# Pool layer of an mLSTM/pooling trunk: group mix multiplied into the input weights, input projection by Strassen with 7 products, output projection accumulated over all of K in PSUM

## The chip, the core and the metric

The kernel runs on one core of one Trainium2 chip. The metric is device time in microseconds (us). Of the kernel before there are three timed executions: 1609.27, 1611.42 and 1612.48 us, median 1611.42. One further execution was profiled. It took 1616.39 us, and its span from the first to the last instruction is 1614.3 us. All rows below are from that one.

## What is computed

```python
def _pool_branch(x, w_in, w_group, scale, w_out):      # layer 1; S = D = 1024, E_B = 2048
    proj = x @ w_in                                    # (1024, 1024) @ (1024, 4096)
    u, z = proj[..., :E_B], proj[..., E_B:]
    csum = jnp.cumsum(u, axis=1)
    for gi, win in enumerate((2, 4, 8, 16)):           # 4 groups of 512 channels
        cg = csum[..., gi * CG_B:(gi + 1) * CG_B]
        means.append((cg - prev) / cnt)                # trailing mean over win tokens
    pooled = concatenate(means) - u
    mixed = einsum("bsgc,gcd->bsgd", pooled, w_group) * scale    # 512 x 512 for each group
    return (mixed * silu(z)) @ w_out                   # (1024, 2048) @ (2048, 1024)

# x <- LayerNorm(alpha * x + branch(x)), layer 0 (mLSTM, 8 heads) first, then this one
```

The window mean acts along tokens and the group mix along channels, so the two can change places.

## The kernel before, in words

TensorE works on float32 data in three passes: each operand is split into a rounded part (`_hi`, type fp32r, made by ScalarE) and a remainder (`_lo`, made by GpSimd or VectorE), and `split` (L1388 to L1392) issues hi times hi, lo times hi and hi times lo. So a product of 128 x 128 weights with 512 columns is three matmuls.

Layer 0 (mLSTM) runs head by head. Its last output projection, the LayerNorm between the layers and the first products of the pool layer are interleaved in TensorE's queue by the table `BRIDGE` (L74): T are transposes of the last head's output, O the 16 last output products of layer 0, X the 16 groups of four transposes that bring the normed input back to channels on partitions, U the first two input products.

The pool layer then goes through its four groups (`group`, in the blocks of TensorE, VectorE and ScalarE). For each group TensorE makes 4 + 4 blocks of the input projection (u and z, each 128 channels by 2 x 512 tokens by 8 K tiles), the group mix (`G_MIX`), and the output projection of the group's 512 channels (`project`, L1429), whose partial sums VectorE adds to `acc` in SBUF (L962). Weights arrive in slots of 128 x 1024 floats in a ring of two: DMA to `w_raw`, ScalarE to `w_hi` (L646), GpSimd to `w_lo` (L541). Four PSUM banks (`wide`) rotate. VectorE makes the window sums (L1303: four levels for every group, those not wanted multiplied by a flag of zero), the pooled value (L1310), its remainder (L1315), the gate (L1324) and the gated product (L1337).

The last group's projection goes token tile by token tile. As each tile is done, its LayerNorm passes through VectorE (L1210, L1364), ScalarE (sum of squares L822, scaling L938), GpSimd (L570, L572, L636) and out. The two last tiles are finished by VectorE (L1369).

Each engine's order is the order in which its block of code issues; there is no planner. Waits are semaphores. On VectorE every instruction that feeds the next waits on a semaphore of its own (`step`, `link`).

Of the kernel before, what the change touches and what calls it, by code (L numbers as in the profile page):

```python
# [84 lines left out]
SLOTS_PER_HEAD = 8
SLOT_LAST_OUT = SLOTS_PER_HEAD * HEADS - 2
SLOT_POOL = SLOTS_PER_HEAD * HEADS
SLOTS_PER_GROUP = 14
# [6 lines left out]
G_U, G_Z, G_MIX, G_OUT = 0, (8, 16), (12, 36), (20, 40)  # L95
GS_U, GS_Z, GS_MIX, GS_OUT = 0, (4, 7), (6, 11), (9, 12)
# [12 lines left out]
VEC_BETWEEN, VEC_GROUP = 2, 20  # L109


SET_IDENT, SET_PAR, CONST_SETS = 2, 4, 14
POOL_SETS = 4 + 3 * GROUPS + sum(win - 1 for win in WINDOWS)
LATE = NC - 2
# [32 lines left out]
def group_uses(g):  # L147
    return Uses(g * USES_PER_GROUP + USE_POOL, g * (USES_PER_GROUP // 4) + USE_POOL // 4)


def build(nc, x, w_in, conv_w, conv_b, w_q, w_k, w_v, b_i, b_f, norm_g, skip, w_out,
          p_in, p_group, p_scale, p_out, ln_g, ln_b, out):
    m_rows = nc.dram_tensor("m_rows", (HEADS, S), F32, kind="Internal").ap()
    wc_rows = nc.dram_tensor("wc_rows", (HEADS, NC), F32, kind="Internal").ap()
    with ExitStack() as ctx:
# [17 lines left out]
        sb("line_0", [P, (BASE - CONSTS - SMALLS) // 4])  # L173
        with ExitStack() as behind:
            normed_out = sb("normed_out", [P, NC, D], where=behind)
        x_hi = sb("x_hi", [P, KT, S], F32R)
        x_lo = sb("x_lo", [P, KT, S], F32R)
        acc = sb("acc", [P, NC, D])
        w_raw = sb("w_raw", [P, 2, SLOT])
        w_hi = sb("w_hi", [P, 2, SLOT], F32R)  # L180
        w_lo = sb("w_lo", [P, 2, SLOT], F32R)
        gate_t = sb("gate_t", [P, 2, HALF])


        with ExitStack() as gates:
            e_buf = sb("e_buf", [P, 2, S], where=gates)
            f_buf = sb("f_buf", [P, 2, S], where=gates)
        y_hi = sb("y_hi", [P, 2, S], F32R)
        y_lo = sb("y_lo", [P, 2, S], F32R)


        with ExitStack() as own:
            def sa(name, shape, dt=F32):
                return sb(name, shape, dt, own)
            xm = sa("xm", [P, 2, HALO + S])
            sa("line_1", [P, (LINE - 32) // 4])

            with ExitStack() as whole:
                xc = sb("xc", [P, 2, S], where=whole)
            xc_lo = sa("xc_lo", [P, 2, S], F32R)  # L200
# [178 lines left out]
        def by_feature_tile(k):  # L379
            return bank(k).rearrange("p (f t) -> p f t", f=4)  # L380
# [1280 lines left out]
```

## Time and profile before

| | |
|---|---|
| median of 3 timed executions | 1611.42 us |
| profiled execution, its time | 1616.39 us |
| its span | 1614.3 us |
| PE busy | 1558.9 us (97%) |
| DVE, ACT, POOL busy | 1044.3, 491.4, 429.6 us |
| mean granted TensorE clock | 0.986 |

PE is TensorE, DVE VectorE, ACT ScalarE, POOL GpSimd, SP the engine that issues the transfers. A matmul's record is longer than its share of the engine, because matmuls overlap: how fast TensorE goes is read from the distance between starts. Records carry start, duration, engine, line, output, inputs; brackets give the idle time before and what ended it. A granted clock of 1 is 2.4 GHz, and half of it 1.2 GHz.

### The profile page before, as it was taken

The page shows a single profiled execution, that of the slowest core. Times are in us where ns is not written, and L with a number is a line of the kernel's source. Part 1 is how long each engine was busy: PE and PEld are TensorE (multiplying, and loading weights), DVE is VectorE, ACT ScalarE, POOL GpSimd, SP SyncE. Part 2 cuts the span into 40 slices and gives each one's busy share as a digit, 9 for nine tenths or more (in the row PEclk, how much of TensorE's full clock was granted, in tenths as well). Part 3 has the DMA queues.
Part 4 walks back from the last instruction along what each step waited for, and adds up shares of the span by engine and source line. Part 5 has one row for each costly group of instructions (what it writes and reads, how often), then busy time and mean ns, then how long its engine had stood idle before and what let it go on. Part 6 is the DMA issues. An engine that isn't in the chain of part 4 may idle for free.

```text
span 1614.3 us, 20693 instructions
## 1 busy us (share of the span) xinstructions
PE 1558.9 (97%) x7186; PEld 1295.1 (80%) x7186; DVE 1044.3 (65%) x1507; ACT 491.4 (30%) x711; POOL 429.6 (27%) x260
## 2 busy tenths in 40 slices
PE   7999999999999999999999879899999999999995
PEld 6888888888888888888888758678888888888884
DVE  4868757567577477576675787855563565348348
ACT  4632332422422332323224243221221123112214
POOL 2203202213122123132032153452122222212226
PEclk8999999999999999999999999999999999999998
DMA  5112111201112112021111021111111111111113
GB/s 173 47 34 64 42 40 52 60 31 52 52 30 61 39 39 65 26 65 50 28 52 52 0 66 40 39 53 40 53 53 49 43 52 52 39 52 52 41 50 119
DMA packets 108509, 82.59 MB, mean 51 GB/s; under 512 B 4120, under 2 KB 96424, under 8 KB 108464
## 3 DMA queue, kind: packets, MB, share of 16 engines
q1 hardware_dynamic: 107392, 81.94, 17.1%
q8 instruction: 26, 0.43, 0.1%
q10 hardware_dynamic: 1072, 0.07, 0.0%
q14 instruction: 19, 0.16, 0.0%
HBM read 77.77 MB, written 4.23 MB: 51 GB/s over the span
## 4 chain that ended last, share of the span: by engine, by line
PE 85%; DVE 11%; ACT 1%; issue 1%; DMA 1%; POOL 1%; DVEq 0%; SPq 0%; ACTq 0%; POOLq 0%
PE wide L1390 26%; PE wide L1391 26%; PE wide L1392 26%; PE ps_intra L1540 2%; PE ps_state L1545 1%; PE ps_inter L1543 1%; DVE win_b L1303 1%; DVE normed_out L1364 1%; PE wide L1447 1%; PE ps_s L1533 1%; DVE acc L1291 1%; DVE win_a L1303 1%; DVE tmp_a L1048 1%; DVE acc L1210 1%; DVE x_lo L969 0%
## 5 line engine op out<-in xcount | busy, mean ns | idle before, releaser
L541 POOL TENSOR_TENSOR w_lo<-w_raw,w_hi 128x1024 fp32r<-128x1024 f32 x120 | 311.7, 2597 | 854.0 <-ACT w_hi L646 852.6
L1390 PE MATMUL wide<-x_hi,w_hi 128*128 128x512 f32 x1280 | 507.5, 396 | 10.1 <-POOL w_lo L541 10.1
L1392 PE MATMUL wide<-x_hi,w_lo 128*128 128x512 f32 x1280 | 500.6, 391 | 0.0
L1391 PE MATMUL wide<-x_lo,w_hi 128*128 128x512 f32 x1280 | 500.0, 391 | 0.0
L1390 PEld LDWEIGHTS wide<-x_hi,w_hi 128*128 128x128 f32 x1280 | 241.3, 189 | 59.0 <-POOL w_lo L541 11.2
L1392 PEld LDWEIGHTS wide<-x_hi,w_lo 128*128 128x128 f32 x1280 | 241.0, 188 | 50.8
L1391 PEld LDWEIGHTS wide<-x_lo,w_hi 128*128 128x128 f32 x1280 | 241.2, 188 | 47.9
L962 DVE TENSOR_TENSOR acc<-wide,acc 128x512 f32<-128x512 f32 x224 | 154.8, 691 | 98.7 <-PE wide L1392 86.0
L1390 PE MATMUL wide<-w_hi,y_hi 128*128 128x512 f32 x512 | 202.2, 395 | 10.7 <-DVE y_lo L1032 4.8
L1391 PE MATMUL wide<-w_lo,y_hi 128*128 128x512 f32 x512 | 200.8, 392 | 0.0
L1392 PE MATMUL wide<-w_hi,y_lo 128*128 128x512 f32 x512 | 200.7, 392 | 0.0
L646 ACT ACTIVATE w_hi<-w_raw 128x1024 fp32r<-128x1024 f32 x120 | 127.4, 1062 | 186.8 <-PE wide L1392 179.2
L1390 PEld LDWEIGHTS wide<-w_hi,y_hi 128*128 128x128 f32 x512 | 97.0, 189 | 34.4 <-DVE acc L1210 6.5
L1392 PEld LDWEIGHTS wide<-w_hi,y_lo 128*128 128x128 f32 x512 | 97.0, 189 | 20.6
L1391 PEld LDWEIGHTS wide<-w_lo,y_hi 128*128 128x128 f32 x512 | 96.9, 189 | 19.7
L547 POOL TENSOR_TENSOR rstd<-small,nhalf 128x4 f32<-128x4 f32 x16 | 16.1, 1009 | 281.5 <-DVE small L1137 281.5
L1048 DVE SCALAR_TENSOR_TENSOR tmp_a<-xm,cols,tmp_a 128x1024 f32<-128x1024 f32 x48 | 72.0, 1500 | 5.6 <-DVE acc L962 0.3
L1324 DVE SCALAR_TENSOR_TENSOR zz<-gate_t,wide 128x512 f32<-128x512 f32 x32 | 22.0, 687 | 82.0 <-ACT gate_t L882 81.2
L1303 DVE SCALAR_TENSOR_TENSOR win_b<-win_a,flag 128x1024 f32<-128x1024 f32 x32 | 73.1, 2284 | 1.6 <-DVE win_a L1303 0.2
L802 ACT ACTIVATE num<-ps_intra 128x257 f32<-128x257 f32 x64 | 24.8, 387 | 107.1 <-PE ps_state L1545 78.7
L1390 PE MATMUL wide<-p_hi,w_hi 128*128 128x512 f32 x128 | 50.4, 394 | 2.2 <-DVE zz L1324 2.2
L724 ACT ACTIVATE tmp_c<-tmp_a 128x1024 f32<-128x1024 f32 x16 | 17.0, 1062 | 116.8 <-DVE tmp_a L1048 116.8
(182 smaller groups left out, 1967.6 us busy)
## 6 DMA issues: line engine op xcount, KB each, us to landing
w_raw<-in_mlstm_w_in SPq DMA_DIRECT2D x48, 512.0 KB, 3.8
w_raw<-in_pool_w_in SPq DMA_DIRECT2D x32, 512.0 KB, 3.8
w_raw<-in_mlstm_w_out SPq DMA_DIRECT2D x16, 512.0 KB, 3.8
w_raw<-in_pool_w_out SPq DMA_DIRECT2D x16, 512.0 KB, 3.8
acc<-in_x SPq DMA_DIRECT2D x8, 512.0 KB, 6.0
m_bc<-m_rows SPq DMA_DIRECT2D x8, 512.0 KB, 4.7
w_raw<-in_pool_w_group SPq DMA_DIRECT2D x8, 512.0 KB, 3.4
out<-normed_out SPq DMA_DIRECT2D x6, 512.0 KB, 2.6
```

The costliest lines, as they stand in the source:

```text
L541: link(pool, pool.tensor_tensor(w_lo[:, k % 2, :], w_raw[:, k % 2, :], w_hi[:, k % 2, :].bitcast(F32), ALU.subtract), lo_ready, s + 1)
L646: link(act, act.activation(w_hi[:, k % 2, :], w_raw[:, k % 2, :], ACT.Copy), hi_ready, s + 1)
L724: link(act, act.activation(tmp_c[:, :], tmp_a[:, :], ACT.Tanh), conv_tanh, h * 2 + (j + 1))
L802: link(act, act.activation(num[:, c, :], ps_intra[:, 0:DV + 1], ACT.Copy), intra_taken, h * NC + (c + 1))
L962: link_taken(dve, dve.tensor_tensor(acc[:, t, half(n)], bank(k), acc[:, t, half(n)], ALU.add), uses, k)
L1048: ins = dve.scalar_tensor_tensor(out=tmp_a[:, :], in0=xm[:, j, w:w + S], scalar=col(h * 2 + (COL_W + w * ET + j)), in1=tmp_a[:, :], op0=AL ...
L1303: step(dve.scalar_tensor_tensor(out=dst[:, PAD:PAD + S], in0=src[:, back:back + S], scalar=flag[:, bass.ds(g * GROUPS + level, 1)], in1=sr ...
L1324: link_taken(dve, dve.scalar_tensor_tensor(out=zz[:, m // 2, half(m % 2)], in0=gate_t[:, m % 2, :], scalar=1.0, in1=bank(k), op0=ALU.add, ...
L1390: pe.matmul(dst, a[0], b[0], start=first, stop=False)
L1391: pe.matmul(dst, a[0], b[1], start=False, stop=False)
L1392: return pe.matmul(dst, a[1], b[0], start=False, stop=last)
L1540: mm = pe.matmul(ps_intra[:, 0:DV + 1], sT[:, :], v_sb[:, c, :], start=True, stop=True)
```

## The change

1. The group mix is not applied to the pooled data any more. Between the layers TensorE multiplies each group's u part of `pool_w_in` by `w_group` (32 steps "F" of 12 matmuls). The result is evicted by ScalarE to `stage` and written to a DRAM tensor `folded`. The F steps stand in a new `BRIDGE` table between T, O and X.
2. The input projection, u with folded weights and z as before, is 16 pairs of 256 channels by 1024 tokens by K = 1024, each a 2 x 2 block product by Strassen's scheme: 7 products of 12 matmuls in place of 8. Odd pairs are u, even ones z. The sums of weight blocks are made by GpSimd (4 additions of 128 x 512 for each pair), those of x blocks by VectorE, once. M1 (q = 1) is accumulated on in its bank, with copies (snapshots) taken by ScalarE; VectorE joins a second bank to a copy three times for each pair.
3. The window sums take as many levels as the window needs (1 to 4), without a flag. The gated y goes to DRAM (`y_rows`) and comes back by token halves.
4. The output projection runs after all pairs, with all 16 K tiles accumulated in PSUM: 4 token tiles, then 3, then the last one alone with both operands resident. The LayerNorm after it is on VectorE, with only the square root on GpSimd.

The core of the diff:

```diff
+BRIDGE = [("T", 0), ("T", 1), ("F", 0), ("F", 1), ("F", 2), ("T", 2), ("T", 3), *(("O", i) for i in range(8)), ("F", 3),
+          *(("O", i) for i in range(8, 12)), ("X", 0), ("X", 1), ("O", 12), ("X", 2), ...
+PRODUCTS = [(0, 1), (0, 2), (0, 6), (0, 7), (0, 5),
+            *((p - back, q) for p in range(1, PAIRS)
+              for back, q in ((0, 1), (1, 3), (0, 2), (1, 4), (0, 6), (0, 7), (0, 5))),
+            (PAIRS - 1, 3), (PAIRS - 1, 4)]
...
 @block.gpsimd
+            fold_low(3)
+            for t in range(2):
+                deviation(t, 0)
+            fold_low(4)
+            for t in range(2, 4):
+                deviation(t, 0)
...
+            def add(dst, a, b, n):
+                link(pool, pool.tensor_tensor(dst, a, b, ALU.add), added, n)
+            for p in range(PAIRS):
...
+                add(blk_sum_at(AT[p, 7]), a_part(p, 0), a_part(p, 2), 4 * p + 1)
+                add(blk_sum_at(AT[p, 6]), blk_sum_at(AT[p, 7]), a_part(p, 3), 4 * p + 2)
+                pool.wait_ge(blk_lo, AT[p, 2] + 1)
+                add(a_part(p, 1), blk_sum_at(AT[p, 6]), a_part(p, 1), 4 * p + 3)
...
+                add(blk_sum_at(AT[p, 5]), a_part(p, 2), a_part(p, 3), 4 * p + 4)
 @block.scalar
+            for t in range(3):
                 sum_squares(t, 0, squares_a)
...
+            for c in range(4):
+                fold_take(0, c)
+            sum_squares(3, 0, squares_a)
+            for s in (4, 5):
+                fold_high(s)
 @block.vector
+            def join(p, q):
...
+                dve.tensor_tensor(dst, wide[:, at, :], dst, op).then_inc(done, 1)
...
+            def windows_at(t):
+                for p in range(1, PAIRS, 2):
+                    start = AT[p, 3] - 1
+                    ops = p // 4 + 4
+                    for j in range(2):
+                        for n in range(ops):
+                            if start + 2 + 4 * j + n * 5 // ops == t:
+                                window(p, j, n)
...
+            for t in range(TICKS):
+                tick(t)
+            for t in range(TICKS, TICKS + RING + 2):
+                windows_at(t)
...
+            for k in range(ET):
+                wo_low(k)
+                y_low(k)
 @block.tensor
+            def fold_free(b, c):
+                if b == 0:
...
+                elif b in (1, 3):
+                    by, count = formed(4 * b + c)
+                    pe.wait_ge(x1_taken[by], count)
+            def bank_ready(p, q):
+                if q == 1 and p >= 2:
...
+                elif q in (6, 5, 3):
+                    pe.wait_ge(snap, 3 * p + {6: 1, 5: 2, 3: 3}[q])
+                elif q == 2 and p:
+                    pe.wait_ge(c11, p)
+                elif q == 7 and p:
+                    pe.wait_ge(c21, p)
+                elif q == 4:
+                    pe.wait_ge(c22, p + 1)
+            for i, (p, q) in enumerate(PRODUCTS):
+                pe.wait_ge(blk_lo, i + 1)
...
+            for v in range(2 * ET):
+                k, ts = v % ET, range(4, LATE) if v >= ET else range(4)
+                if v < ET:
+                    pe.wait_ge(wo_lo, k + 1)
+                pe.wait_ge(y_half_lo, v + 1)
```

Three places in the queues, first GpSimd between the layers. L570 and L572 (before) and L782 and L784 (now) are the two steps of one token tile's LayerNorm deviation. Before, small memsets stand between them:

```order
L570 TENSOR_SCALAR small<-small 128x1 [waits ln_squares,pool_set]
L572 TENSOR_TENSOR rstd<-small,nhalf 128x1 [waits ln_var]
L589 MEMSET head_fix 128x1 [waits ln_rstd]
L589 MEMSET head_fix 128x1 [waits pool_set] x8
L570 TENSOR_SCALAR small<-small 128x1 [waits ln_squares,pool_set]
```

Now, for tiles 0 to 3:

```order
L782 TENSOR_SCALAR small<-small 128x1 [waits ln_squares,fold_lo0]
L784 TENSOR_TENSOR rstd<-small,nhalf 128x1 [waits ln_var]
L782 TENSOR_SCALAR small<-small 128x1 [waits ln_squares,ln_rstd]
L784 TENSOR_TENSOR rstd<-small,nhalf 128x1 [waits ln_var]
L754 TENSOR_TENSOR fold_w<-fold_raw,fold_w 128x1024 [waits fold_hi,ln_rstd]
L782 TENSOR_SCALAR small<-small 128x1 [waits ln_squares,fold_lo0]
```

A remainder of fold weights (fold 4), which waits for ScalarE, now stands ahead of the deviations of tiles 2 and 3.

Next ScalarE at the same time. Before, with L822 the sum of squares of a token tile, L711 the rounding of the last head's y, L831 the eviction of an X step, L843 its rounding, L646 the rounding of a weight slot:

```order
L822 ACTIVATE tmp_a,small<-acc,small 128x1024 x2
L711 ACTIVATE y_hi<-tmp_c 128x512 x2
L822 ACTIVATE tmp_a,small<-acc,small 128x1024 x4
L831 ACTIVATE x_new<-ps_s,cols 128x512
L843 ACTIVATE x_hi<-x_new 128x512 x4
L646 ACTIVATE w_hi<-w_raw 128x1024
```

Now. L1041 is the sum of squares of a token tile (three, then one), L1072 the eviction of the first four fold tiles, L932 the rounding of fold weights (folds 4 and 5):

```order
L1041 ACTIVATE tmp_a,small<-acc,small 128x1024 x3
L1072 ACTIVATE stage<-ps_s 128x512
L1072 ACTIVATE stage<-ps_intra 128x512
L1072 ACTIVATE stage<-ps_inter 128x512
L1072 ACTIVATE stage<-ps_state 128x512
L1041 ACTIVATE tmp_a,small<-acc,small 128x1024
L932 ACTIVATE fold_w<-fold_raw 128x1024 x2
```

The rounding for fold 4 has come to stand behind the fold evictions and behind the sum of squares of tile 3.

Last VectorE where a group's data becomes ready for the output projection. Before (the last group, second half): the gated products and their remainders, and straight behind them the gate of the next z blocks and the additions of TensorE's projection:

```order
L1032 TENSOR_TENSOR y_lo<-y_t,y_hi 128x512 [waits y_rounded,wide_taken2]
L1337 SCALAR_TENSOR_TENSOR y_t<-wide,cols,zz 128x512 [waits wide_full,y_ready]
L1032 TENSOR_TENSOR y_lo<-y_t,y_hi 128x512 [waits y_rounded,wide_taken3]
L1032 TENSOR_TENSOR y_lo<-y_t,y_hi 128x512 [waits y_rounded,y_ready]
L1324 SCALAR_TENSOR_TENSOR zz<-gate_t,wide 128x512 [waits z_tanh,y_ready]
```

Now, behind the last product and its `join`, the second half of the windows of pair 15 (L1620 sums, L1624 first tokens, L1626 pooled, L1633 gated; the first half, the same seven, stands ahead of it), and then the first remainders of the output projection's weights (L1671) and of y (L1677):

```order
L1620 TENSOR_TENSOR win_a<-u_buf 128x1024 [waits c22,c21,y_made]
L1620 TENSOR_TENSOR win_b<-win_a 128x1024 [waits vec_step]
L1620 TENSOR_TENSOR win_a<-win_b 128x1024 [waits vec_step]
L1620 TENSOR_TENSOR win_b<-win_a 128x1024 [waits vec_step]
L1624 TENSOR_TENSOR win_b<-win_b,head_fix 128x16 [waits vec_step]
L1626 SCALAR_TENSOR_TENSOR win_a<-win_b,u_buf 128x1024 [waits vec_step]
L1633 SCALAR_TENSOR_TENSOR zz<-win_a,cols,zz 128x1024 [waits gate_used,pooled]
L1671 TENSOR_TENSOR wo<-wo_raw,wo 128x1024 [waits wo_hi,y_made]
L1677 TENSOR_TENSOR blk<-blk_raw,blk 128x512 [waits y_half_hi]
```

The operands of the first output product have come to stand behind the last pair's 14 window instructions.

## Rows read from the trace of the kernel before

**Rows 1.** The page: busy time, share of the span, instructions.
```profile
PE 1558.9 (97%) x7186; PEld 1295.1 (80%) x7186; DVE 1044.3 (65%) x1507; ACT 491.4 (30%) x711; POOL 429.6 (27%) x260
```

**Rows 2.** Windows from head 7's end: PE, PEld, DVE, ACT, POOL busy, clock, DMA, GB/s.
```profile
917.25:1057.00 139.75, 114.94 (x501) 92.40 (x502) 116.52 (x140) 47.35 (x67) 64.24 (x81) 0.93 0.15 45
1057.00:1574.00 517.00, 517.00 (x2281) 427.48 (x2279) 274.63 (x289) 115.14 (x144) 129.50 (x52) 1.00 0.16 48
1574.00:1614.30 40.30, 21.84 (x85) 16.52 (x84) 35.71 (x53) 16.84 (x22) 27.08 (x23) 0.82 0.30 119
```

**Rows 3.** PE timeline, start and duration in us, around the layers' border.
```profile
917.25 1.09 PE L1447 MATMUL wide<-ident,num 128*128 128x128 f32 x8 [0.38 <-DVE num L1144]
923.11 0.77 PE L1390 MATMUL wide<-w_hi,y_hi 128*128 128x512 f32 x1 [4.77 <-DVE y_lo L1032]
923.67 0.63 PE L1391 MATMUL wide<-w_lo,y_hi 128*128 128x512 f32 x1
...
927.09 0.44 PE L1390 MATMUL wide<-w_hi,y_hi 128*128 128x512 f32 x1
...
1017.41 0.50 PE L1390 MATMUL wide<-x_hi,w_hi 128*128 128x512 f32 x1 [3.11 <-POOL w_lo L541]
```

**Rows 4.** PE timeline: two X steps (four transposes each), and the last matmul.
```profile
954.70 0.60 PE L1576 MATMUL ps_intra<-ident,acc 128*128 128x128 f32 x4
955.13 0.60 PE L1576 MATMUL ps_inter<-ident,acc 128*128 128x128 f32 x4
...
1599.54 0.39 PE L1392 MATMUL wide<-w_hi,y_lo 128*128 128x512 f32 x1
```

**Rows 5.** Groups by line: count, busy us, mean ns, idle before. DVE.
```profile
L962 DVE TENSOR_TENSOR acc<-wide,acc 128x512 f32<-128x512 f32 x224 | 154.8, 691 | 98.7 <-PE wide L1392 86.0
L1303 DVE SCALAR_TENSOR_TENSOR win_b<-win_a,flag 128x1024 f32<-128x1024 f32 x32 | 73.1, 2284 | 1.6 <-DVE win_a L1303 0.2
L1094 DVE TENSOR_TENSOR xc_lo<-xc,xc_hi 128x1024 fp32r<-128x1024 f32 x16 | 19.6, 1225 | 0.5
```

**Rows 6.** Groups by line, POOL and ACT.
```profile
L541 POOL TENSOR_TENSOR w_lo<-w_raw,w_hi 128x1024 fp32r<-128x1024 f32 x120 | 311.7, 2597 | 854.0 <-ACT w_hi L646 852.6
L596 POOL TENSOR_TENSOR x_lo<-x_new,x_hi 128x512 fp32r<-128x512 f32 x8 | 10.8, 1349 | 8.9 <-ACT x_hi L843 8.7
L646 ACT ACTIVATE w_hi<-w_raw 128x1024 fp32r<-128x1024 f32 x120 | 127.4, 1062 | 186.8 <-PE wide L1392 179.2
L822 ACT ACTIVATE tmp_a<-acc,small 128x1024 f32<-128x1024 f32 x8 | 9.2, 1153 | 15.7 <-DVE small L1216 15.6
```

**Rows 7.** VectorE's timeline in group 0.
```profile
989.29 3.30 DVE L1303 SCALAR_TENSOR_TENSOR win_b<-win_a,flag 128x1024 f32<-128x1024 f32 x1
992.62 1.29 DVE L1303 SCALAR_TENSOR_TENSOR win_a<-win_b,flag 128x1024 f32<-128x1024 f32 x1
```

**Rows 8.** GpSimd's timeline: one deviation between the layers, and the same stretch.
```profile
932.73 0.19 POOL L570 TENSOR_SCALAR small<-small 128x1 f32<-128x1 f32 x1 [5.20 <-ACT tmp_a L822]
933.00 0.56 POOL L572 TENSOR_TENSOR rstd<-small,nhalf 128x1 f32<-128x1 f32 x1
...
989.06 2.44 POOL L541 TENSOR_TENSOR w_lo<-w_raw,w_hi 128x1024 fp32r<-128x1024 f32 x1 [6.17 <-ACT w_hi L646]
```

**Rows 9.** VectorE's timeline between the layers, and its last record.
```profile
927.83 1.76 DVE L1144 TENSOR_SCALAR num<-num,mv,small 128x256 f32<-128x256 f32 x4
...
1608.77 3.12 DVE L1369 SCALAR_TENSOR_TENSOR normed_out<-normed_out,rstd,b_bc 128x512 f32<-128x512 f32 x4
```

**Rows 10.** DMA issues: size, median us from issue to landing.
```profile
w_raw<-in_mlstm_w_in SPq DMA_DIRECT2D x48, 512.0 KB, 3.8
acc<-in_x SPq DMA_DIRECT2D x8, 512.0 KB, 6.0
out<-normed_out SPq DMA_DIRECT2D x4, 256.0 KB, 2.0
```

More of the change, by code:

```diff
@@ L108, with by_vector, fold_count @@
 VEC_START, VEC_FIRST, VEC_LATER = 4, 68, 58
[L109 to L114, printed above, removed]
+SET_IDENT, SET_PAR = 2, 4
+CONST_SETS = 14
+FIX_SETS = GROUPS + sum(win - 1 for win in WINDOWS)
+LATE = NC - 1
+def by_vector(s):
+    return s > 12 and s % 2 == 1
+def fold_count(s):
+    return sum(by_vector(i) == by_vector(s) for i in range(s + 1))
 def formed(n):
@@ L172, in build, with at_kb @@
         small = sb("small", [P, 4, NC])
[L173 to L189, printed above, removed]
+        head_fix = sb("head_fix", [P, GROUPS, PAD])
+        sb("line", [P, (BASE - CONSTS - SMALLS) // 4])
+        def at_kb(where, name, taken, kb):
+            assert taken <= kb * KB
+            sb(name, [P, int(kb * KB - taken) // 4], where=where)
         with ExitStack() as own:
@@ L564, in head @@
                     make_lo(s0 + (at["slots"] + f), f)
+                if last:
+                    for s in range(3):
+                        fold_low(s)
                 powers(1)
@@ new lines, in _ @@
+            dve.wait_ge(gb_last_in, 32)
+            for v in range(ET + AHEAD, 2 * ET):
+                y_low(v)
+                t = v - ET - AHEAD - 1
+                if 0 <= t < 4:
+                    norm_out(t)
+            for t in range(4, LATE):
+                for n in range(2):
+                    residual_in(2 * t + n, t, n)
+                mean(t, NC)
+            for t in range(4, LATE):
+                norm_out(t)
+            for n in range(2):
+                residual_in(2 * LATE + n, LATE, n)
+                step(dve.bn_stats(stats[:, n, :], acc[:, LATE, half(n)]))
@@ new lines, in _ @@
+            for i, (p, q) in enumerate(PRODUCTS):
+                pe.wait_ge(blk_lo, i + 1)
+                if i < 2:
+                    pe.wait_ge(x0_lo, 4 * i + 4)
+                elif p == 0:
+                    pe.wait_ge(x_lo_done, X_WAIT[q])
+                bank_ready(p, q)
+                dst = wide[:, {2: 2, 7: 3, 4: 3}.get(q, p % 2), :]
+                for t in range(4):
+                    mm = split(dst, [v[:, tile(t)] for v in (blk_hi_at(i), blk_lo_at(i))],
+                               [v[:, t, :] for v in operands[q]], t == 0 and q in (1, 2, 7), t == 3, q not in (1, 2, 7))
+                mm.then_inc(prod, 1)
```

1158 lines of the change are left out of this document (725 added, 433 removed).

## The prediction

> **What bounds the kernel now.** I read the page first: PE is busy 97% of the span, no other engine above 65% [rows 1]. So time is saved by fewer matmuls or by filling the places where PE waits. The windows by stage say where those are. I cut at 917.25, where the last head's products of layer 0 end; what lies before it the change leaves as it is, apart from some small GpSimd memsets and three early fold roundings that have cover. The middle stretch, 517 us, is full: 2281 matmuls, all but a few of 512 columns, or 0.2267 us each. The border between the layers (139.75 us) and the end (40.3 us) are not [rows 2]. From 917.25 to the end of the span are 697.05 us. TensorE's work in them: 2688 matmuls of the pool layer (1536 input, 384 mix, 768 output) at 0.2267 = 609.4; 96 of the last output products of layer 0 = 21.8; 16 X steps at 0.43 = 6.9 and 2.2 for the T transposes [rows 3, 4]; together 640.3. The last matmul ends near 1599.7, so 14.6 us are the tail behind it [rows 4]. The rest, 697.05 - 640.3 - 14.6 = 42.2, is waiting and half clock. The timeline shows both: 4.77 us of waiting at 923.11, and behind it nine matmuls 0.43 us apart (923.67 to 927.09, granted clock at its lower level, 1.2 GHz), which costs 9 x 0.2 = 1.8 us more. The wait of 3.11 us before 1017.41 was not followed by that [rows 3]. I price a wait of over 2 us with 1.3 us of clock on top, between the two.
>
> **The matmuls removed.** The group mix costs the same in both places: 32 F steps of 12 = 384 matmuls, because tokens and model width are both 1024. Output 768, as before. Input 112 products of 12 = 1344 in place of 1536. So 192 matmuls go: 192 x 0.2267 = **-43.5 us**.
> The Trainium skill, page "TensorE: Matmul & The Clock Gate", section "Wait — 56ns, not 53.3ns?", has 215.7 ns for a warm matmul of 512 columns; by it the saving would be 41.4 us. The trace does not agree for these operands, and its 0.2267 is used.
>
> **The border, new waits.** T0, T1 and F0 to F2 now cover the wait at 923.11 and end at 917.25 + 1.1 + 8.2 = 926.6; but T2 needs the second half of the normed output, ready at 927.83 + 1.76 = 929.6 [rows 9]: wait 3.0. Then T2, T3, eight O (10.9), F3 (2.7), four O (5.4): 949.9, where X0 stands. It needs token tiles 0 to 3 normed. GpSimd's queue has the remainder of fold 4 ahead of the deviations of tiles 2 and 3, and this waits for ScalarE, which first evicts F3 (to 945.2), then makes the sum of squares of tile 3 (1.15) and the rounding (1.06) [rows 6]: 947.5. GpSimd 2.6 more, two deviations of 0.19 + 0.56 [rows 8], and on VectorE a norm, two additions and a norm behind them (some 2.6): X0 at 954.4, wait 4.5. Queued behind that GpSimd instruction are both deviations, and all of TensorE waits for them. Around X8 to X15 ScalarE must evict block 2, round folds 14 and 15 and form X8 before X12 can overwrite its bank; fold 15 is fetched only when two evictions are done, lands 3.8 later [rows 10], is rounded in 1.06, and form X8 and X12 follow: some 7 us from the end of F11 to F12, with 3.4 of work in them: wait 4. The remaining F steps have four slots: landing 3.8 + rounding 1.06 + remainder 2.6 + use 2.72 + 0.6 of semaphores = 10.8 for the 10.9 us that four F steps take. That just holds; I give 0.6 us for each of seven blocks, 4.5. Sum 16.0, with clock for three of them 3.9: **19.9 us**.
>
> **The products.** PE needs 2.72 us for each of 112. VectorE's load for two pairs (38.1 us of PE): 14 remainders, 6 joins, 4 gates at 0.73 (0.69 and a gap) = 17.5, and the windows of the u pair: for each half g+1 sums at 1.27, 0.2 for the first tokens, two instructions at 1.32 [rows 5]. That is 25.7, 28.2, 30.8 and 33.3 us for groups 0 to 3: below 38.1, so on average it has room. But PE waits at one tight place: product (p+1, M7) overwrites the bank that `join` of (p, M4) reads, and only one product stands between. For z pairs this join is behind the windows. Counting VectorE's queue from the end of (p, M5) to that join, group 2: 4.6 + 2.7 + 3.1 + 2.8 + 0.7 = 14.0 us against 5 products = 13.6. One sum less for group 1, two for group 0; group 3 has 15.2. And in this stretch GpSimd makes its four additions of 1.3 us [rows 6].
> What does an addition cost VectorE? The window sum at 989.29 took 3.30 us where the next took 1.29; GpSimd was at a remainder from 989.06 to 991.50, and VectorE ended 1.09 behind that [rows 7, 8]. Over 32 such instructions the mean is 2284 ns [rows 5]. The additions that read PSUM keep 691 in the mean of 224 [rows 5]: these are not held. So bounds: none held, waits in all seven z pairs 0, 0, 0, 0, 0.4, 0.4, 1.6 = 2.4; all four held (5.2 us), 3.0, 3.0, 4.3, 4.3, 5.6, 5.6, 6.8 = 32.6. I take three of four held (3.9 us), since rows 7 show a full hold where VectorE is busy without a gap and one addition meets a join: 1.7 + 1.7 + 3.0 + 3.0 + 4.3 + 4.3 + 5.5 = 23.5. Clock for five of them 6.5; start of the stage (last fold stored, then blocks 4 and 5) 1.5: **31.5 us**.
> The Trainium skill, page "SBUF — State Buffer", section "Terms", says that VectorE and GpSimd share a port pair, that it is locked for the whole instruction and that the loser fully blocks. The trace agrees at 989.29. Taken for every addition it gives the upper end, which is a rival below.
>
> **Between products and output projection.** VectorE's queue holds, from the last product on: a join 0.73, 14 window instructions of pair 15 (8 x 1.27 + 2 x 0.2 + 4 x 1.32 = 15.9), then the first remainder of the output weights 1.27 and of y 0.73. TensorE waits for both, and nothing else is left for it: 18.6 + 0.3 + clock 1.3 = **20.2 us**. Bounds: GpSimd is silent here, so these are the unheld times; 17 to 22.
>
> **Output projection.** For each K tile TensorE takes 5.4 us; VectorE 1.27 + 0.73 + 2.6 (residual gain) = 4.6, ScalarE 1.06 + 0.63. PE stays full. The y tiles 14 and 15 are needed 76 us later. Nothing is late in the second half either. The 256 additions to `acc` that go (L962) were off the path.
>
> **The tail.** Before, it is bound by VectorE: each token tile there takes two additions and an L1364 of some 2.4 us, and VectorE is still at 1608.77 + 3.12 [rows 9]. Now only tile 7 is left: addition, statistics, variance, four normings of 128 x 512 at 0.69 to 0.78, some 5 us, and a transfer of 2.0 [rows 10] with 0.6 around: 7.6. **-7.0 us**.
>
> **Sum.** New waits 19.9 + 31.5 + 20.2 = 71.6 in place of 42.2: +29.4. -43.5 + 29.4 - 7.0 = -21.1. The profiled execution took 1616.39 (span 1614.3 and 2.1 around it), so 1595.3 on its scale. It stood 5.0 above the median of the runs, 1611.42; on their scale the forecast is **1590 us**.
>
> **Rivals.**
> A, the holds are hidden: GpSimd's additions fall where VectorE idles or reads PSUM. For it: VectorE has 5 to 12 us of room in two pairs. Against: the additions are released right at the window burst. Products wait 2.4, no clock there: 23.5 - 2.4 + 6.5 = 27.6 less, 1562.
> B, every addition holds VectorE in full: 32.6 and clock 9: 11.6 more, 1602.
> C, slower than before: the F steps are paced by their transfers. For it: loads of x with four in flight land in 6.0 us [rows 10], F steps need 512 KB every 2.72 us, and each block's stores go through the same queue, whose load of every fourth fold waits for two evictions. Chain 6.0 + 7.0 = 13.0 for four steps of 10.9: 2.1 x 7 = 15, and the queue's late fourth load 1.3 x 7 = 9 more: +24 and clock 2, 1616. It decides from a landing of about 4.0 us on. Against: before, 512 KB loads in the steady state land in 3.8.
> D, the change does not do what it says: PE does not keep 0.2267 in the products, since 12 matmuls alternate among four banks with seven waits for each pair, and 0.02 more on each of the 1344 eats 27 us: 1617. Rows 2 speak against it; before too a bank changed every 6 to 24 matmuls.
>
> **Chances.** Forecast 0.48, A 0.18, B 0.20, C 0.09, D 0.05. A difference below 0.2% (3.2 us) can't be told from none. Forecast and A are faster; of B and of the forecast's upper side a little reaches 1608; C and D split between no change and slower. Faster 0.84, same 0.06, slower 0.10. The range reaches from A's time to the upper side of B and the near side of C: 1562 to 1612.
>
> **What would show it.** In the profile of the changed kernel: one PE wait of 18 to 20 us ended by VectorE just ahead of the output projection; waits of 2 to 6 us ended by a VectorE join, once in every two pairs, growing with the group; GpSimd additions of 1.3 us beside window sums of over 2 us; X0 held some 4 us by a norm of VectorE; PE starts 0.2267 apart elsewhere; 8 us from the last matmul to the end. I am wrong if the products go without waits (A), if F steps wait for roundings one after the other (C), or if a wait that I have not priced stands before a stage, such as the first products waiting for x combinations.

## The result and the profile after

The changed kernel takes **1625.11 us** (median of 8 runs, 1616.91 to 1628.08), the kernel before 1610.66 beside it (8 runs, 1609.27 to 1614.52). The ratio is 1.0078, 95% interval 1.0058 to 1.0098: slower by 0.8%, where 1590 and faster had been forecast, and outside the range of 1562 to 1612. The profiled execution took 1626.17 us with a span of 1624.4; the forecast span was 1614.3 - 21.1 = 1593.2. So 31.2 us have to be explained.

First the page of the changed kernel, its busy lines (compare [rows 1]), and then windows of the same trace, cut at the first T step, the first product, the last product's end and the first output matmul. Their columns are those of [rows 2].

```profile
PE 1527.4 (94%) x6994; PEld 1265.0 (78%) x6994; DVE 1057.3 (65%) x1559; ACT 568.5 (35%) x850; POOL 385.9 (24%) x259
```
```profile
914.18:1090.95 176.77, 135.68 (x560) 108.43 (x561) 106.47 (x130) 84.61 (x109) 70.64 (x43) 0.86 0.45 137
1090.95:1422.63 331.68, 313.84 (x1345) 255.59 (x1343) 223.00 (x261) 124.39 (x201) 94.78 (x65) 0.98 0.25 83
1422.63:1441.06 18.43, 0.16 (x2) 0.03 (x1) 17.75 (x18) 9.41 (x11) 0.00 (x0) 0.62 0.98 398
1441.06:1624.40 183.34, 175.89 (x768) 144.93 (x768) 92.18 (x124) 34.91 (x50) 8.29 (x15) 0.98 0.20 69
```

The 192 matmuls are gone, 7186 - 6994, and yet the span grew. The third window is the bubble ahead of the output projection, with no work for TensorE. The first is the one that surprised: TensorE's work in it is 117.9 us by the durations of before, so 58.9 are lost, where 19.9 were forecast. Stage by stage against the prediction:

| | forecast | measured |
|---|---|---|
| layer 0 up to the first T step | 917.25 | 914.18 (-3.1) |
| lost at the border | 19.9 | 176.8 - 117.9 = 58.9 (+39.0) |
| lost in the products | 31.5 | 331.7 - 304.6 = 27.0 (-4.5) |
| bubble, with its clock | 20.2 | 18.4, and 1.6 of clock in the output stage (-0.2) |
| tail behind the last matmul | 7.6 | 7.6 |

-3.1 + 39.0 - 4.5 - 0.2 = +31.2. The miss lies wholly at the border. This is what TensorE waited for from the first T step on (line and operand waited for, total us, times, longest):

```profile
PE ps_s L1755 <- DVE blk L1677: 18.3, 1, 18.3
PE wide L1755 <- DVE zz L1594: 15.7, 7, 4.2
PE ps_s L1755 <- DVE fold_w L1511: 13.8, 2, 7.9
PE ps_s L1755 <- POOL fold_w L754: 10.7, 5, 6.2
PE ps_s L1936 <- DVE acc L1492: 5.4, 1, 5.4
PE ps_s L1936 <- ACT xa_raw L1048: 3.9, 1, 3.9
PE ps_s L1936 <- ACT stage L1072: 3.3, 1, 3.3
PE wide L1804 <- DVE num L1408: 3.2, 2, 2.8
...
```

The first two lines are the bubble and the seven joins, in the places that were forecast; the bubble has its size too (18.9 forecast), the joins are a third smaller (23.5). X0 (5.4 for 4.5) and T2 (2.8 for 3.0) are there too. Two lines hold what I had not priced: 13.8 us in two F steps that wait for VectorE, and 6.2 us of the fourth line at F0. What is left of that line, 4.5 us in four F steps, is as much as was forecast for the F steps.

**The two F steps.** The two are F27, which starts at 1064.25, and F29 at 1080.00. The chain that ended last runs to both by the same kinds of steps; here is its last step ahead of F27 and its part ahead of F29 (start, us, what):

```profile
1060.95 3.25 DVE fold_w L1511
...
1069.33 4.54 DMA fold_raw<-in_pool_w_fold
1073.96 1.06 ACT fold_w L932
1075.05 1.06 ACT xb L1066
1076.20 1.24 DVE xa L1533
...
1078.72 1.23 DVE fold_w L1511
1080.00 0.80 PE ps_s L1755
```

And VectorE's own timeline around the second of them, with its idle time in brackets:

```profile
1076.20 2.48 DVE L1533 TENSOR_TENSOR xa<-xa_raw,xb 128x1024 fp32r<-128x1024 f32 x2 [12.01 <-ACT xb L1066]
1078.72 1.22 DVE L1511 TENSOR_TENSOR fold_w<-fold_raw,fold_w 128x1024 fp32r<-128x1024 f32 x1
```

VectorE stood idle for 12.01 us with the remainder of fold 29 behind it in its queue, whose rounding ScalarE had ended at 1067.67. Ahead of that remainder stood two remainders of x combinations, the sums of x blocks that only the products need (`combined_lo`, L1533). They waited for `combined_hi` (L1066) of the same block, which stood in ScalarE's queue behind the rounding of fold 31, and that waited for a load issued at 1069.3. So the weight that TensorE needed next waited for a weight two steps further on, by way of an operand that no F step uses. Ahead of F27 the remainder itself took 3.25 us where that of F29 took 1.22: it ran beside one of GpSimd's (2.47 us from 1060.64), so some 2 of the 5.90 us are that hold. A chain that starts at a load can be read as "the transfers are the bound" (my rival C) or as "the order is" - the first two experiments were made to tell these apart.

**F0 and T2.** First VectorE, then GpSimd, behind the first T step at 914.18:

```profile
919.21 5.50 DVE L1296 TENSOR_TENSOR y_lo<-tmp_c,y_hi 128x512 fp32r<-128x512 f32 x2
...
925.20 2.30 DVE L1455 SCALAR_TENSOR_TENSOR e_buf<-gate_t,e_buf 128x512 f32<-128x512 f32 x1
...
930.26 2.37 DVE L1406 TENSOR_TENSOR small<-small,rstd 128x4 f32<-128x4 f32 x1 [1.25 <-POOL rstd L750]
932.66 1.77 DVE L1408 TENSOR_SCALAR num<-num,mv,small 128x256 f32<-128x256 f32 x4
```
```profile
916.13 2.49 POOL L744 TENSOR_TENSOR w_lo<-w_raw,w_hi 128x1024 fp32r<-128x1024 f32 x1 [7.17 <-ACT w_hi L857]
918.70 8.26 POOL L754 TENSOR_TENSOR fold_w<-fold_raw,fold_w 128x1024 fp32r<-128x1024 f32 x3
...
930.24 2.37 POOL L754 TENSOR_TENSOR fold_w<-fold_raw,fold_w 128x1024 fp32r<-128x1024 f32 x1
```

F0's remainder stands behind that of the last output slot (L744), which ScalarE rounds only after the last chunk of tokens of head 7. So F0 to F2 did not cover the wait for T2: they had one of 6.16 us of their own. And the norm that T2 needs came later than before: 932.66 + 1.77, 20.3 us behind the first T step, where it was 12.3 [rows 3, 9]. VectorE's rows show why. Two remainders of 512 columns took 5.50 us (1.49 in undisturbed places), one of 0.69 took 2.30, and an instruction of 128 x 4 took 2.37 for 0.16: each beside a remainder of GpSimd, the added ones among them.

### The profile page after: what moved, and what is told of

It is laid out like the page before. It is cut to its first block, busy times and chain, and to the rows that moved or that the text cites. A ratio compares the mean times of both kernels' runs of the same rounds, so it can differ in the third digit from the quotient of the medians.

```text
span 1624.4 us, 20438 instructions
## 1 busy us (share of the span) xinstructions
PE 1527.4 (94%) x6994; PEld 1265.0 (78%) x6994; DVE 1057.3 (65%) x1559; ACT 568.5 (35%) x850; POOL 385.9 (24%) x259
## 4 chain that ended last, share of the span: by engine, by line
PE 80%; DVE 12%; ACT 3%; DMA 2%; issue 2%; POOL 1%; SPq 0%; DVEq 0%; ACTq 0%; POOLq 0%
PE wide L1755 22%; PE wide L1757 21%; PE wide L1756 21%; DMA fold_raw<-in_pool_w_fold 2%; PE ps_intra L1897 2%; PE ps_inter L1900 1%; PE ps_state L1902 1%; DVE blk L1574 1%; DVE win_a L1620 1%; PE wide L1804 1%; DVE win_b L1620 1%; PE ps_s L1890 1%; PE ps_s L1755 1%; DVE tmp_a L1312 1%; ACT fold_w L932 1%
## 5 line engine op out<-in xcount | busy, mean ns | idle before, releaser
L1755 PE MATMUL wide<-x_hi,w_hi 128*128 128x512 f32 x768 | 307.1, 400 | 0.0
L1757 PE MATMUL wide<-x_hi,w_lo 128*128 128x512 f32 x768 | 299.7, 390 | 0.0
L1756 PE MATMUL wide<-x_lo,w_hi 128*128 128x512 f32 x768 | 298.8, 389 | 0.0
L744 POOL TENSOR_TENSOR w_lo<-w_raw,w_hi 128x1024 fp32r<-128x1024 f32 x64 | 168.3, 2629 | 422.4 <-ACT w_hi L857 421.3
L1757 PEld LDWEIGHTS wide<-x_hi,w_lo 128*128 128x128 f32 x768 | 144.1, 188 | 31.2
L1756 PE MATMUL wide<-xa,blk 128*128 128x512 f32 x384 | 149.4, 389 | 0.0
L1755 PE MATMUL wide<-xb,blk 128*128 128x512 f32 x320 | 127.9, 400 | 17.8 <-DVE zz L1594 15.7
L1757 PE MATMUL wide<-xb,blk 128*128 128x512 f32 x320 | 127.1, 397 | 0.0
L1755 PE MATMUL wide<-w_hi,y_hi 128*128 128x512 f32 x256 | 101.2, 395 | 0.0
L1756 PE MATMUL wide<-w_lo,y_hi 128*128 128x512 f32 x256 | 100.8, 394 | 0.0
L1757 PE MATMUL wide<-w_hi,y_lo 128*128 128x512 f32 x256 | 100.7, 393 | 0.0
L1755 PEld LDWEIGHTS wide<-xb,blk 128*128 128x128 f32 x320 | 61.7, 193 | 35.0 <-issue 20.6
L750 POOL TENSOR_TENSOR rstd<-small,nhalf 128x4 f32<-128x4 f32 x16 | 16.1, 1009 | 279.2 <-DVE small L1401 279.2
L1757 PEld LDWEIGHTS wide<-xb,blk 128*128 128x128 f32 x320 | 61.5, 192 | 13.3
```

Of the source, the lines that this page charges most:

```text
L744: link(pool, pool.tensor_tensor(w_lo[:, k % 2, :], w_raw[:, k % 2, :], w_hi[:, k % 2, :].bitcast(F32), ALU.subtract), lo_ready, s + 1)
L1755: pe.matmul(dst, a[0], b[0], start=first, stop=False, skip_group_check=more)
L1756: pe.matmul(dst, a[0], b[1], start=False, stop=False, skip_group_check=more)
L1757: return pe.matmul(dst, a[1], b[0], start=False, stop=last, skip_group_check=more)
```

## The experiments

Each edit is made on the changed kernel unless it says otherwise. Ratios are to the kernel before, with 95% intervals; the changed kernel's is 1.0078. In the traces the part of layer 0 before the border ended anywhere from 910.8 to 915.7 us where no edit touched it, so I compare stretches: border (first T step to first product), products, and bubble. In the changed kernel these are 176.8, 331.5 and 18.7 us (from start to start of a matmul). The border itself moves too: in the three runs below that leave it alone (`fills`, `spread`, `bubble`) it took 172.8, 173.9 and 173.9. So 3 to 4 us of a difference to 176.8 can be chance.

**e1_vec: VectorE's order at the border.**
```
-    elif i < 18: combined_lo(i - 8)
+    elif i < 12: combined_lo(i - 8)
+ if s == 27: combined_lo(4); combined_lo(5)
+ (behind fold_low(31):) for n in range(6, 10): combined_lo(n)
```


> Only VectorE's order in the border is changed: combined_lo(4) and (5) stand behind fold_low(27), combined_lo(6) to (9) behind fold_low(31). The same work, the same loads, stores and ScalarE order. Theory 1 (VectorE's queue is blocked: the remainder of a fold that TensorE is waiting for stands behind remainders of x combinations, whose roundings stand behind a later fold's rounding on ScalarE, which waits for its load): the PE waits of 5.90 us at 1064.25 and 7.94 at 1080.00 shrink to under 1.5 each, the half clock behind them goes, first product some 14 us earlier (1090.95 to about 1077), time 1625 to about 1611. Theory 2 (my rival C: the F steps are paced by the landing of their loads, 4.2 to 5.8 us): the loads are the same, so the waits only move between F steps, and less than 3 us are won.

1613.87 us, ratio 1.0007 (0.9987 to 1.0027). Border 161.2, 15.6 us less (and 12.7 less than the untouched 173.9). Theory 1 holds. The waits of 5.90 and 7.94 are gone (next to the same places 0.54 and 1.73 us are left), with loads and landings as they were (median 4.4 us in both). A wait of 3.14 at the first product came instead: its block remainder now stands behind four `combined_lo`. Rival C falls. These are all of TensorE's waits between 1040 and 1075 us of that trace:

```profile
1045.72 0.50 PE L1760 MATMUL ps_s<-fold_w 128*128 128x512 f32 x1 [0.54 <-POOL fold_w L754]
1058.94 0.50 PE L1760 MATMUL ps_s<-fold_w 128*128 128x512 f32 x1 [1.73 <-POOL fold_w L754]
1073.27 0.50 PE L1760 MATMUL wide<-xa,blk 128*128 128x512 f32 x1 [3.14 <-DVE blk L1574]
```

**e1_act: the same knot cut on ScalarE.**
```
 for b in range(1, FOLDS // 4):
+    (3 <= b < 7:) combined_hi(n)          # its n as before
     for c in range(4): ... fold_take(b, c)
     for s in (4b+6, 4b+7): fold_high(s)
-    (3 <= b < 7:) combined_hi(n)
```


> Only ScalarE's order in the border is changed: the roundings of the x combinations (combined_hi) of a block stand ahead of its evictions and of the next fold roundings, in place of behind them. VectorE's order is that of the changed kernel. Theory 1 (queue blocked by way of ScalarE): as combined_lo no longer waits for a load, the waits at 1064.25 and 1080.00 fall from 13.8 us together to under 3, and the time to about 1611 to 1613, as with VectorE's order alone. Theory 2 (landing of the loads paces the F steps): within 3 us of 1625.

1610.27 us, ratio 1.0003 (0.9988 to 1.0018). Border 161.6, 15.2 less, though VectorE's order is the changed kernel's; the waits of 5.90 and 7.94 are gone here too. One wait grew to 3.41 (a fold's rounding now stands behind four `combined_hi`, 4.3 us). Either cut undoes the knot, so it is shown as the cause of the 13.8 us.

**dev: the deviations of tiles 2 and 3 ahead of fold 4 on GpSimd.**
```
-fold_low(4)
 for t in range(2, 4): deviation(t, 0)
+fold_low(4)
```


> Only GpSimd's queue: the deviations of tiles 2 and 3 stand ahead of the remainder of fold 4, which waits for ScalarE's rounding behind the block's evictions. Theory 1 (X0 waits 5.42 us because of that order): the wait falls to about 1, as in the kernel with all orders changed, gain 4.3 + 1.3 of clock, time about 1619 to 1620. Theory 2 (the normed tiles are late by VectorE's own chain): under 1 us won.

1616.86 us, ratio 1.0023 (1.0008 to 1.0037). X0 waits 1.20 for 5.42; border 168.3, 8.5 less. That is more than expected, but only 4.2 of it is X0's wait: T2's wait was 1.0 shorter in this run and the two of the knot 1.2 together, and untouched borders differ by as much.

**first and early: folds 0 to 2.** In `first` GpSimd makes their remainders ahead of that of the last output slot; in `early` ScalarE rounds them at chunks 1 to 3 and GpSimd makes them ahead of its first power (L750, the step that turns a head's variances into the factors of its norms):
```
first:  make_lo(slots); fold_low(0..2); make_lo(slots + 1); powers(1)
early:  fold_low(0..2); powers(0); make_lo(slots); make_lo(slots + 1); powers(1)
        if last and c in (1, 2, 3): fold_high(c - 1)      # was (4, 5, 6): c - 4
```


> Only GpSimd's queue: the remainders of folds 0 to 2 stand ahead of that of the second last output slot, whose rounding ScalarE makes after the last decay. Theory 1 (F0 waited 6.16 us because its remainder stood behind that one): F0 starts right behind T1, F0 to F2 then cover that stretch; T2's wait for the normed output stays and may grow from 2.8 to 4; the gain is 4 to 5 us with the clock, time about 1620. Theory 2 (the folds' own rounding or load is late): wait unchanged, 1625.

1626.25 us, ratio 1.0091 (1.0064 to 1.0119): nothing won. F0's wait went as theory 1 had it, but T0 got one of 5.79 in its place, which neither theory had. VectorE and GpSimd of that run:
```profile
917.18 6.00 DVE L1408 TENSOR_SCALAR num<-num,mv,small 128x256 f32<-128x256 f32 x4
```
```profile
911.96 7.59 POOL L754 TENSOR_TENSOR fold_w<-fold_raw,fold_w 128x1024 fp32r<-128x1024 f32 x3
919.79 2.34 POOL L744 TENSOR_TENSOR w_lo<-w_raw,w_hi 128x1024 fp32r<-128x1024 f32 x1 [0.24 <-ACT w_hi L857]
```
The four norms that T0 needs took 6.00 us beside these remainders, where they took 1.76 in the changed kernel.

> Against the changed kernel, ScalarE rounds folds 0 to 2 at chunks 1 to 3 of the last head in place of 4 to 6, and GpSimd makes their remainders ahead of its first power and of the last output slots. GpSimd had 32 us of idle time there. Where they stand in the changed kernel (or, in the run with GpSimd's order changed alone, 3 us sooner) they run beside VectorE's norms of the last head, which took 6.0 us for four in place of 1.8, and the wait only changed its name from F0 to T0. Theory 1 (GpSimd's remainders slow VectorE, so that only moving them out from beside the norms helps): the 6.16 us wait at F0 goes and T0 does not wait in its place; T2 still waits some 3; gain 6 + 2 of clock, time about 1617. Theory 2 (the holds only move into the chunks, whose VectorE chain TensorE follows): new waits of over 0.5 us inside the last head, time within 3 of 1625.

1620.02 us, ratio 1.0051 (1.0032 to 1.0069). F0 follows T1 without a wait and T0 waits as in the changed kernel (0.4); border 170.5, 6.3 less. T2's wait rose to 5.33: its norm still comes late, at 930.04, because GpSimd's fold 3 starts with the last power and holds it. combo2 and combo4b below hold that one back too, and T2 then waits 3.1, what the prediction had.

**fills and spread: the joins in the products.** `fills` lets GpSimd fill each sum's target with a constant from pair 2 on, which leaves these sums out; `spread` only moves window instructions:
```
fills:   ins = pool.memset(dst, 0.01) if n > 8 else pool.tensor_tensor(dst, a, b, ALU.add)
spread: -start + 2 + 4 * j + n * 5 // ops == t
        +start + 2 + 6 * j + n * 4 // ops == t
        (and the loop over the last window ticks runs one tick longer)
```


> From pair 2 on GpSimd fills the target of each sum with a constant in place of adding two blocks; these sums are left out, the number of its instructions and what they wait for is the same. Theory 1 (GpSimd's additions slow VectorE's SBUF instructions beside them: near 1249 us a window sum took 2.20 us in place of 1.22, a gate 1.67 for 0.60 and a remainder 1.77 for 0.60, 3.2 us together, and so the z pairs' join comes late): the seven PE waits ended by a VectorE join, 15.7 us together, fall to under 3 us; with their clock the time is about 1625 - 12 - 4 = 1609. Theory 2 (VectorE's queue of windows is too long there by itself): they keep 12 of 15.7 us, time within 3 us of 1625.

1604.08 us, ratio 0.9950 (0.9937 to 0.9963). The seven joins cost 1.3 us in place of 15.7 and products take 309.9. GpSimd's fill takes 0.53 us (a sum 1.3 to 2.3), and it does not disturb VectorE. Here are two groups of VectorE in the changed kernel (1150 to 1410 us) and the same two in `fills` (1150 to 1400):
```profile
L1574 DVE TENSOR_TENSOR blk<-blk_raw,blk 128x512 fp32r<-128x512 f32 x39 | 36.9, 973 | 20.3 <-POOL a_raw L819 19.4
L1620 DVE TENSOR_TENSOR win_a<-u_buf 128x1024 f32<-128x1024 f32 x12 | 19.5, 1626 | 0.2
```
```profile
L1575 DVE TENSOR_TENSOR blk<-blk_raw,blk 128x512 fp32r<-128x512 f32 x36 | 24.3, 690 | 26.0 <-ACT blk L1085 25.8
L1621 DVE TENSOR_TENSOR win_a<-u_buf 128x1024 f32<-128x1024 f32 x13 | 15.9, 1221 | 0.2
```


> The window instructions of the second half of a u pair come two ticks later (ticks 8 to 11 behind the start in place of 6 to 10), those of the first half within four ticks; the same instructions, GpSimd unchanged. By a count of VectorE's queue with 3.2 us of slowing for each pair of additions, the join of (z pair, M4) is then in time for every group. Theory 1 (the queue between the join of M5 and that of M4, made longer by GpSimd): the seven waits fall from 15.7 to under 3, time about 1609, though the end of the last window and with it the 18.3 us wait ahead of the output projection stay or grow by up to 1.5. Theory 2 (the join waits for ScalarE's snapshot or tanh and not for VectorE's own queue): the waits stay, time within 3 of 1625.

1605.97 us, ratio 0.9975 (0.9958 to 0.9992). The joins cost 4.4 us in three places, products take 313.6, with GpSimd's sums as they were. So both halves of the reading hold: the wait is VectorE's queue between two joins, and GpSimd is what makes this queue too long. `fills` also shortens GpSimd's own path to the blocks, so its last few us need not all be the hold.

**bubble: the output remainders woven with the last windows.**
```
-for t in range(TICKS, TICKS + RING + 2): windows_at(t)
 for k in range(ET):
     wo_low(k); y_low(k)
+    for t in (TICKS + 2*k, TICKS + 2*k + 1): windows_at(t)
-    if 2 <= k < 2 + NC: gain(k - 2)
+    if 6 <= k < 6 + NC: gain(k - 6)
```


> VectorE's queue at the end of the products is woven: the remainders of the first output weight and of y 0 stand ahead of the window instructions of pair 15, two ticks of these follow each K tile, and the eight residual gains start four K tiles later. The same work. Theory 1 (the 18.3 us wait ahead of the output projection is VectorE's queue alone): it falls to under 4 us, no new wait over 1 us behind it, time 1625 - 15 - 2 of clock = about 1608. Theory 2 (something else would be late next, such as the load of the first output weights, 10.7 us in landing, or VectorE's load in the first K tiles): more than half of it comes back, time over 1615.

1611.98 us, ratio 1.0006 (0.9994 to 1.0018). The bubble is 5.5 for 18.7, and the output stage behind it takes 176.6 for 175.5. The wait left is 5.13: one join, two window sums and two remainders. So the wait was VectorE's queue (theory 1), and 13.1 of the 17 us expected came.

**combo1 to combo4b: all orders together.** combo1 has e1_act, first, dev, bubble and spread, and two more:
```
DVE:  ... fold_low(31); block_lo(0..3); combined_lo(6..9); block_lo(4..5)
ACT:  (b = 2, behind fold_take(2, 3):) form_x(8); fold_high(14); form_x(12); fold_high(15)
```


> All orders changed together: x combinations' roundings ahead on ScalarE, their remainders behind the last folds' on VectorE (four of them behind the first four block remainders), windows spread, output remainders woven with the last windows, GpSimd's folds 0 to 2 ahead of the last slot, the deviations of tiles 2 and 3 ahead of fold 4, and form X8 and X12 ahead of the roundings of folds 14 and 15. If each wait is its own queue's (theory 1), the gains add: 15 border, 13 before the output projection, 15 to 20 in the products, 4 at F0, 3 at X0, 3 at X12: 1625 - 53 to 58, about 1570. If TensorE's lost time is given back elsewhere (theory 2: the engines behind it are as loaded as it is, so that a wait removed comes back as another), over 1585.

1571.20 us, ratio 0.9756 (0.9730 to 0.9781): the gains add. Border 143.6 (from T0's start, which still waits 5.8), products 315.3, bubble 5.5.

combo2 has in place of some of these (combo3 is the same without early):
```
POOL: early; wait for the last norms ahead of fold_low(3)
ACT:  fold_take(2, 0..3); form_x(8); fold_high(12..13); form_x(12); fold_high(14..15)
ACT:  fold_high(4b+6); combined_hi (two); fold_high(4b+7)         # b = 3 to 5
ACT:  block_hi(0..1); combined_hi(6..9); block_hi(2..3)           # b = 7
DVE:  start + 1 + 6 * j + n * 5 // ops; wo_low(0), y_low(0) ahead of the last join
SP:   load_y(0) ahead of load_wo(4), load_wo(5)
ACT:  the last two ticks behind the rounding of output weight 0
```


> The kernel with all orders changed (1571.2), with six further moves: folds 0 to 2 early as in the run named early; fold 3's remainder only when the last head's norms are done; the evictions of block 2 and form X8 ahead of the roundings of folds 12 and 13; the x combinations' roundings between those of folds 4b+6 and 4b+7, where ScalarE waits for a load; window instructions one tick sooner; the first output remainders ahead of the last join and y 0 loaded before two output weights. Theory 1 (what is left of the waits is each one queue's order): T0 5.8, T2 1.9, X8 3.3, F28 3.3, 4.4 in the products and 5.1 ahead of the output projection fall to some 7 together, 17 us with clock, time about 1554 to 1558. Theory 2 (they come back elsewhere): over 1566.

> As combo2, but folds 0 to 2 are rounded and their remainders made where the changed kernel makes them. The difference between the two is the price of GpSimd's three remainders beside VectorE's norms in a kernel whose other waits are gone. Theory 1: 6 to 8 us above combo2, with F0 waiting 6 us. Theory 2 (the holds move into the chunks): no difference.

combo2 1559.86 us, ratio 0.9666 (0.9642 to 0.9691); combo3 1564.82, ratio 0.9695 (0.9668 to 0.9722). Their difference is 5.0 us, a little under the 6 to 8 expected; F0 waits 6.17 in combo3 and not in combo2, and T2 3.1 in combo2 for 0.9. Two moves of my own did harm in both: the third product (called product 4 in the next expectation) waited 6.0 and 5.4 us, and with windows a tick sooner the products took 324.7 and 324.9. So the six moves gave 11 where 17 were expected.

combo4b mends both:
```
ACT:  (b = 7:) block_hi(0..3); fold_take(7, 0..3); combined_hi(6..9)
DVE:  start + 2 + 6 * j + n * 4 // ops
```


> The kernel named combo2 (1559.9) with two places mended that its trace shows: the four last x combinations' roundings stood on ScalarE ahead of block roundings 2 and 3 and of the last evictions, so product 4 waited 6.0 us; they now stand behind the last evictions, where ScalarE waits for a store. And the window instructions are back to ticks 2 to 5 and 8 to 11, which lost less (112 products in 313.6 us, as in the run named spread, in place of 324.7). Theory 1 (queue order is all that is left there): product 4 waits some 1.3, products take 314 to 316, the time is 1560 - 9 = about 1551. Theory 2 (product 4 waits for the landing of the last folds' store, 4.4 us, whatever the order): 1555 to 1557.

**1549.57 us** (5 runs, 1546.17 to 1551.73), ratio **0.9610** (0.9597 to 0.9623), faster than both kernels. Border 132.7, products 316.0, 0.4 ahead of the output. That is theory 1, though the third product still waits 2.2 and not 1.3. The largest of TensorE's waits from 905 us on, and then the window of the border:
```profile
PE wide L1777 <- DVE zz L1613: 4.4, 3, 2.5
PE wide L1826 <- DVE num L1420: 3.5, 2, 3.2
PE ps_s L1777 <- POOL fold_w L755: 3.1, 3, 1.5
PE wide L1777 <- ACT zz L1138: 2.2, 1, 2.2
PE ps_s L1777 <- ACT xa_raw L1050: 1.2, 1, 1.2
...
```
```profile
912.26:1044.99 132.73, 123.37 (x560) 98.70 (x561) 102.63 (x125) 80.46 (x105) 64.08 (x40) 0.99 0.58 183
```
The same folds go through the same queue at 183 GB/s (137 in the changed kernel's border), the clock is at 0.99 for 0.86, and landing takes 4.3 us. Loads that land in 4.3 us can thus feed the F steps with 3.1 us of waits for their weights; rival C had put the limit at about 4.0.

## Why the prediction was wrong

- **Matmuls removed, -43.5: right.** 192 went. In `fills`, 112 products took 309.9 us with 3.4 of waits and 1.0 of half clock in them: 305.5, against 304.6 by the old 0.2267 per matmul. So rival D falls too.
- **Border, 19.9: the step that failed, by 39.0.** Four parts. (1) *"The remaining F steps"*: I followed transfer, rounding, remainder and use of a fold round its ring, and put 0.6 us on each of seven blocks. This sum was right in size for the ring (seven times 0.6 is 4.2 and not 4.5; measured 4.5, in four waits and not in seven, so the match is partly luck) but left out that VectorE's and ScalarE's queues carry the x combinations between the folds: 13.8 us in two waits, shown by two cuts. My own warning, *"a wait that I have not priced"*, named x combinations but at the first products, where I looked only for their readiness and not for what they block. (2) *"F0 to F2 now cover the wait"*: they stood behind the last output slot's remainder, 6.2 us. (3) *Clock, 3.9*: 58 matmul starts in the border stood at 0.3 to 0.7 us, 11.1 us over the full rate, because there were seven waits above 2 us and not three. I had 1.3 us for each, and 11.1 / 7 = 1.6; it was the count above all. (4) X8 and X12 cost 7.3 for 4, X0 5.4 for 4.5. (1) to (4) make 13.8 + 6.2 + 7.2 + 4.2 = 31.4. The other 7.6 are small: two waits of 0.54, 1.6 us in all at the first matmul behind ten of the waits, 4.4 in the X transposes, which were 0.18 us apart where 0.11 was counted, and 0.6 spread over the rest.
- **T2, 3.0: right in size and wrong in its working.** Its norm was 8 us later than before, and F0's unpriced wait hid most of that. With both mended it is 3.1.
- **Products, 31.5: the mechanism right, 27.0 measured.** The main term was a third too high: the joins were 15.7 for 23.5. Clock (7.0 for 6.5) and the start of the stage (1.3 for 1.5) were as forecast; a wait of 0.8 for a snapshot and 2.2 of small losses had no price and made up for part of it. The seven waits were 0.97, 0.97, 1.82, 1.82, 2.96, 2.96, 4.22, forecast 1.7 to 5.5 in the same pairs. My price of GpSimd's sums was too high: VectorE lost some 3.2 us for each four and not 3.9 (2.20 + 1.67 + 1.77 for 1.22 + 0.60 + 0.60), since the sums themselves were stretched, to 2.3 and 2.2 us from 1.3. VectorE and GpSimd in e1_vec, where no other work differs:
```profile
1248.96 2.20 DVE L1625 TENSOR_TENSOR win_a<-u_buf 128x1024 f32<-128x1024 f32 x1
1251.19 1.67 DVE L1603 SCALAR_TENSOR_TENSOR zz<-gate_b,zz 128x512 f32<-128x512 f32 x1
1252.79 1.77 DVE L1574 TENSOR_TENSOR blk<-blk_raw,blk 128x512 fp32r<-128x512 f32 x1
```
```profile
1247.76 2.32 POOL L819 TENSOR_TENSOR blk_raw<-blk_raw,a_raw 128x512 f32<-128x512 f32 x1
1250.15 2.16 POOL L819 TENSOR_TENSOR a_raw<-blk_raw,a_raw 128x512 f32<-128x512 f32 x1
```
- **Bubble, 20.2: right,** 18.3 of waiting and 1.6 of clock. **Output full: right. Tail: right,** 7.6.
- **Rivals.** A falls: the joins did wait, and stopped with GpSimd's sums gone. B's mechanism is there in part. D (1617) and C (1616) ended nearest in time, neither by its cause: with loads unchanged, the waits that C meant left with the order. The probability was set wrong too: the 0.10 for slower came from C and D, none from a queue knot, though the change put new instructions on all five queues between the layers.

The Trainium skill, page "SBUF — State Buffer", section "🔬 SBUF: two separate sides", says that the port pair shared by VectorE and GpSimd is locked by whichever starts first, for its whole instruction, against a VectorE instruction with two SBUF inputs or in a two-port mode, the former only where GpSimd reads SBUF. The runs agree with the last condition, as GpSimd's fills left VectorE at 690 ns where sums made it 973. In the `first` run norms with one data input in SBUF went from 1.76 to 6.00 us for four, as the two-port case would have it; no run shows which mode they ran in. I had used this rule for the products and not for the border, where GpSimd's instruction, a remainder of 128x1024, is twice as long (2.4 to 2.7 us for 1.3).

## What to carry to other kernels

Before an operand's preparation is put into a queue, ask for each entry which one behind it is needed sooner; a remainder that waits for something late holds all that follows, and the knot can run over two engines and a load. Three F steps of cover are worth nothing if what they need stands behind the event that they are to cover. The change takes away 2.7% of the matmuls; as first ordered it cost 0.8% of time, and with the moves of combo4b it gave 3.9%. Nearly all of these moves could be read from one wait and the idle rows of the engine named in it. The kernel before was given no such moves, so the 3.9% is not the worth of the change alone.

## What the runs showed of the hardware

- A GpSimd remainder of 128x1024 made VectorE instructions wait that have one SBUF input (four norms 6.00 for 1.76 us) or only four columns (2.37 for 0.16); those that read PSUM kept 0.48 and 0.69, and a statistics instruction with one SBUF input (L1450, 128x256) kept 0.43 beside the same remainders. A GpSimd fill of 128x512 took 0.53 us and held nothing: window sums beside one kept 1.21 to 1.23.
- GpSimd is stretched as well: sums of 1.29 us took 2.32 and 2.16 beside a busy VectorE.
- With the waits at the border cut from 41.1 to 8.9 us, its mean granted clock rose from 0.86 to 0.99, and starts over 0.3 us apart cost 3.6 for 11.1 us. So between these two kernels each us of waiting taken away gave 1 + 7.5 / 32.2 = 1.23 us.
